# A one-core diffusion layer with 32 streamed experts: reordered and halved weight loads, gate rows moved into the routing, a split first gather, and VectorE's round test moved

## The reference, cut to what matters

```python
h = rmsnorm(x) * (1 + sc_m) + sh_m
mix = mixing_branches(h, ...)
x = x + gt_m * mix
h = rmsnorm(x) * (1 + sc_f) + sh_f
logits = h @ w_router + b_router
g = softmax over the 4 largest of the 32 logits
for e in range(32):
    gate, up = split(h @ w_up[e] + b_up[e])
    y = ((clip(up) + 1) * min(gate, 7) * sigmoid(1.702 * gate)) @ w_down[e] + b_down[e]
    acc += g[:, e] * y
x = x + gt_f * acc
y = rmsnorm(x) * g_final
```

## Time and profile before

| | us |
|---|---|
| runs | 1147.65 median of 3 (1145.46 to 1150.6) |
| the profiled execution | 1146.25 |
| its span, first to last instruction | 1144.4 |
| PE busy in the span | 1070.3 (94%) |
| DVE busy | 332.1 (29%) |
| ACT busy | 169.8 (15%) |
| moved by DMA | 459.37 MB, mean 401 GB/s |

### The profile page before, as it was taken

The page is one execution under the profiler, slowest core; times in us unless marked ns, Lnnn a source line. Parts: engine busy times, 40 slices in busy tenths (PEclk is TensorE's granted clock), DMA queues, the critical chain, the costliest instruction groups (busy, mean ns, idle before and its releaser), DMA issues.

```text
span 1144.4 us, 14105 instructions
## 1 busy us (share of the span) xinstructions
PE 1070.3 (94%) x5882; PEld 505.8 (44%) x5882; DVE 332.1 (29%) x622; ACT 169.8 (15%) x303; POOL 66.4 (6%) x107
## 2 busy tenths in 40 slices
PE   7999899899999999989999999999999999999996
PEld 6877699843333333333333333333333333333332
DVE  4775877522121212121212121212121211211113
ACT  4453145411000000000000000000000000000001
POOL 5050000200000000000000000000000000000000
PEclk9999999999999999999999999999999999999999
DMA  9988977899999999998999999999999999999995
GB/s 308 375 253 341 387 271 319 335 409 406 428 427 434 429 434 434 428 431 365 423 440 431 431 435 426 438 424 439 428 434 432 429 438 424 438 424 438 430 421 221
DMA packets 44056, 459.37 MB, mean 401 GB/s; under 512 B 3668, under 2 KB 16024, under 8 KB 26888
## 3 DMA queue, kind: packets, MB, share of 16 engines
q1 hardware_dynamic: 42376, 455.12, 95.4%
q0 software_dynamic: 1168, 2.81, 1.0%
q10 hardware_dynamic: 464, 0.79, 0.2%
HBM read 457.12 MB, written 1.57 MB: 401 GB/s over the span
## 4 chain that ended last, share of the span: by engine, by line
PE 47%; DMA 45%; DVE 3%; SPq 2%; issue 1%; ACT 1%; POOL 1%; POOLq 0%; DVEq 0%; ACTq 0%
DMA arena<-in_w_down_dram 41%; PE ps L1772 21%; PE ps L1733 12%; DMA ring<-in_w_in_dram 3%; PE ps L1761 2%; PE ps L1713 2%; DMA ring<-in_w_ada_dram 1%; DMA ring<-in_rpb_dram 1%; SPq L427 1%; PE ps L1467 1%; PE ps L1468 1%; PE ps L1635 1%; PE ps L1469 1%; SPq L423 1%; PE ps L1637 1%
## 5 line engine op out<-in xcount | busy, mean ns | idle before, releaser
L1733 PE MATMUL ps<-ring,arena 128*64 128x512 f32 x2048 | 455.1, 594 | 1.7 <-ACT arena L850 0.8
L1772 PE MATMUL ps<-arena,x 128*64 128x512 f32 x992 | 236.7, 633 | 44.6 <-DMA arena<-in_w_down_dram 44.6
L1733 PEld LDWEIGHTS ps<-ring,arena 128*64 128x64 f32 x2048 | 142.5, 137 | 270.6 <-issue 255.3
L1772 PEld LDWEIGHTS ps<-arena,x 128*64 128x64 f32 x992 | 74.8, 145 | 205.0 <-issue 151.0
L1278 DVE TENSOR_SCALAR x<-ps 128x512 f32<-128x512 f32 x32 | 22.1, 692 | 254.8 <-PE ps L1733 254.8
L1293 DVE TENSOR_TENSOR late<-ps,gtf 128x512 f32<-128x512 f32 x64 | 41.2, 686 | 187.6 <-PE ps L1772 187.6
L1271 DVE TENSOR_SCALAR arena<-iota,cur 128x128 f32<-128x128 f32 x64 | 19.3, 345 | 259.9 <-PE ps L1743 256.7
L640 POOL COPY selbuf<-sel 96x64 bf16 (+1 forms) x32 | 24.5, 766 | 848.9 <-DVE x L1279 846.5
L1761 PE MATMUL ps<-late,arena 64*128 64x512 f32 x264 | 65.6, 615 | 1.5 <-DVE late L1293 1.5
L1713 PE MATMUL ps<-arena 128*128 128x128 f32 x512 | 62.7, 276 | 0.0
L862 ACT ACTIVATE x<-x 128x512 f32<-128x512 f32 x32 | 20.1, 630 | 283.4 <-DVE x L1278 283.4
(11 more groups left out here) (267 smaller groups left out, 859.6 us busy)
## 6 DMA issues: line engine op xcount, KB each, us to landing
ring<-in_w_up_dram SPq DMA_DIRECT2D x51, 4096.0 KB, 30.9
arena<-in_w_down_dram SPq DMA_DIRECT2D x26, 4096.0 KB, 20.3
ring<-in_w_up_dram SPq DMA_DIRECT2D x26, 2048.0 KB, 11.5
arena<-in_w_down_dram SPq DMA_DIRECT2D x9, 2048.0 KB, 16.9
ring<-in_w_ada_dram SPq DMA_DIRECT2D x16, 1024.0 KB, 10.6
ring<-in_w_ada_dram SPq DMA_DIRECT2D x16, 512.0 KB, 10.1
ring<-in_w_in_dram SPq DMA_DIRECT2D x16, 512.0 KB, 9.5
ring<-in_w_in_dram SPq DMA_DIRECT2D x8, 1024.0 KB, 7.2
```

The lines of the kernel that those rows point to most:

```text
L1733: ins = mm(ps[CAP * h:CAP * h + CAP, half, :].rearrange("q (p j) -> q p j", j=4), xgT[:, place, kk, CAP * a:CAP * a + CAP], w[:, half, :, ...
L1772: ins = mm(ps[CAP * n:CAP * n + CAP, YB, :], hT[:, j, CAP * h:CAP * h + CAP], w[:, jj, n * HALF:(n + 1) * HALF], start=(jj == 0), stop=(jj ...
```

## The change

Five things are changed. (1) `EVEN_FROM` goes from 10 to 24, so the order with ahead = 4 holds up to expert 23; the load loop issues down(6) to down(21) with the up chunks between, and its body is written in that order. `down` of the experts 28 and 29 is loaded in halves too. (2) The first 1 MB row of `up(2)` is issued by itself once `up(0)` has read its row 0 (`row_free`), the second row behind `moe_free`. (3) gt_f is spread during the routing (`spread_gate`, in the place of `inject(0, 0)`, with 64 output columns a matmul, into banks 4 and 7), and ACT copies it in two instructions ahead of the loads of `b_down`; the second half of `down(0)` waits for it, since it overwrites gt_f's rows. (4) The gather ahead of expert 0 is split in two quarters with a copy each, so that row 0 waits for the first alone; `inject(0, 0)` and `inject(1, 0)` stand ahead of `up(1)`. (5) DVE's test for a further round stands ahead of the last `gated`, and the last scatter has a semaphore of its own.

```diff
-EVEN_FROM, EVEN_TO = 10, E - 4
-LOAD_LOOPS = (EVEN_TO - EVEN_FROM) // LOAD_BODY
+LOAD_FROM, LOAD_TO, EVEN_FROM = 6, 22, 24
+LOAD_LOOPS = (LOAD_TO - LOAD_FROM) // LOAD_BODY
-DOWN_HALVES = [0, 1, 2, 3, E_LAST - 1]
+DOWN_HALVES = [0, 1, 2, 3, E_LAST - 3, E_LAST - 2, E_LAST - 1]
...
+                                if (e, c, h) == (2, 0, 0):
+                                    sp.wait_ge(row_free, r + 1)
+                                    sp.dma_start(up_chunk(2, 0)[:, 0, :], w_up_v[2, :, 0, 0:SLOT])\
+                                        .then_inc(up_loaded[0][0], 16)
+                                    sp.wait_ge(moe_free, R + 1)
+                                    sp.dma_start(up_chunk(2, 0)[:, 1, :], w_up_v[2, :, 0, SLOT:2 * SLOT])\
+                                        .then_inc(row_loaded, 16)
+                                    continue
...
                 for h in range(2):
+                    if h and r == 0:
+                        sp.wait_ge(bc_done, 2)
                     down_part(0, 4 * h, 4 * h + 4, down_loaded[h])
-                fixed(order(2, EVEN_FROM + 2))
+                chunks = order(2, E)
+                starts = [chunks.index(("down", e, None)) for e in (LOAD_FROM, LOAD_TO, E - 2)]
+                fixed(chunks[:starts[0]])
                 with sp.Fori(0, LOAD_LOOPS) as i:
...
-                        for c in range(2):
-                            up_whole(e0 + (h + 2), h, c, at0 + 6 * h)
-                        down_whole(e0 + (h + 1), at0 + 6 * (h + 1))
-                fixed(order(EVEN_TO + 2, E)[:-1])
+                        down_whole(e0 + h, at0 + 6 * h)
+                        up_whole(e0 + (h + 2), h, 1, at0 + 6 * h)
+                        up_whole(e0 + (h + 3), 1 - h, 0, at0 + 6 * (h + 1))
+                fixed(chunks[starts[1]:starts[2]])
...
+            def gate_rows_out():
+                act.wait_ge(bc_done, 2)
+                for t in range(2):
+                    ins = nc.scalar.activation(gate_rows[:, t, :], ps[:, GT_BANK[t], :], ACT.Copy)
                 ins.then_inc(bc_read, 1)
...
-            mod_out(0)
...
             nc.scalar.activation(misc[:, 12:13], mhalf[:, :], ACT.Exp)
+            gate_rows_out()
             act.wait_ge(af_t, 4)
...
+                    for h, (done, ready) in enumerate(((gath_first, xg_first), (gath_done, xg_ready))):
+                        act.wait_ge(done, 1)
+                        nc.scalar.activation(xgT[:, 1, 2 * h:2 * h + 2, :],
+                                             ps[:, FIRST[h], 0:2 * P].rearrange("p (a b) -> p a b", a=2),
+                                             ACT.Copy).then_inc(ready, 1)
...
-                gated(R + E - 1, N + PIECES)
...
             further_rounds(dve, more, run)
+            dve.wait_ge(L["gfin"], 16)
+            gated(E - 1, PIECES)
...
-                dve.wait_ge(last_scat, t + 1)
+                dve.wait_ge(final_scat, t + 1)
...
+            def spread_gate():
+                for t in range(2):
+                    for n in range(2):
+                        q = 2 + n
+                        ins = mm(ps[CAP * n:CAP * n + CAP, GT_BANK[t], :], selrow[32 * q:32 * q + 32, t, 0:CAP],
+                                 modrow[32 * q:32 * q + 32, 2, :], start=True, stop=True)
                 ins.then_inc(bc_done, 1)
...
-            spread(0)
...
-            inject(0, 0)
+            spread_gate()
...
             inject(0, 1)
+            pe.wait_ge(bc_read, 2)
             inject(1, 1)
...
+                if r == 0 and e == 1:
+                    inject(0, 0)
+                    inject(1, 0)
...
                         if kk == 0:
+                            pe.wait_ge(xg_first, 1)
+                        if kk == 2:
                             pe.wait_ge(xg_ready, 1)
-                        if kk == 2:
                             pe.wait_ge(h2_ready, 4)
-                            gather(1, 1, FIRST[1])
+                            gather(1, 1, FIRST[2])
                             totals()
                         if kk == 4:
                             pe.wait_ge(xg_ready, 2)
-                            inject(1, 0)
...
-            gather(1, 0, FIRST[0])
+            pe.wait_ge(oh_ready, 1)
+            for h, done in enumerate((gath_first, gath_done)):
+                for j in range(2 * h, 2 * h + 2):
+                    for t in range(2):
+                        ins = mm(ps[:, FIRST[h], (j % 2) * P:(j % 2 + 1) * P], h2[:, t, j * P:(j + 1) * P], oh[:, t, :],
+                                 start=(t == 0), stop=(t == 1))
+                ins.then_inc(done, 1)
```

More of the change, by code:

```diff
@@ L384, in layer_kernel @@
         NT = [(n, t) for n in range(2) for t in range(2)]
-        AF_BANK = (0, 1, 2, 3)
-        FIRST, AGAIN = (6, 3), (2, 3)
+        AF_BANK, GT_BANK = (0, 1, 2, 3), (4, 7)
+        FIRST, AGAIN = (6, 4, 3), (2, 3)
         def read_flags(eng):
@@ L779, in _, with shift_out @@
             pt_out(2)
-            def mod_out(n):
-                act.wait_ge(bc_done, n + 1)
+            def shift_out():
+                act.wait_ge(bc_done, 1)
                 for t in range(2):
[L786 to L793, removed]
+                    ins = nc.scalar.activation(h2[:, t, :].rearrange("p (a j q) -> p a q j", a=2, j=4),
+                                               ps[:, 2 + 2 * t:4 + 2 * t, :].rearrange("p a (q j) -> p a q j", j=4),
+                                               ACT.Copy)
+                ins.then_inc(bc_read, 1)
+            def gate_rows_out():
+                act.wait_ge(bc_done, 2)
+                for t in range(2):
+                    ins = nc.scalar.activation(gate_rows[:, t, :], ps[:, GT_BANK[t], :], ACT.Copy)
                 ins.then_inc(bc_read, 1)
@@ L878, in experts @@
                 R = r * E
-                for c in range(2):
-                    xg_out(R + 1 + c, c, 1, (AGAIN if r else FIRST)[c])
+                if r:
+                    for c in range(2):
+                        xg_out(R + 1 + c, c, 1, AGAIN[c])
+                else:
+                    for h, (done, ready) in enumerate(((gath_first, xg_first), (gath_done, xg_ready))):
[3 more added lines that the diff above has]
+                                             ACT.Copy).then_inc(ready, 1)
+                    xg_out(2, 1, 1, FIRST[2])
                 if r == 0:
@@ L1330, in run @@
             def run(r):
+                gated(r * E - 1, r * PIECES)
                 dve.wait_ge(last_scat, 2 * r)
@@ L1589, in _, with spread_shift @@
             prob_t(Ss[:, :, P:TOK], 4)
[L1591 to L1598, removed]
+            def spread_shift():
+                pe.wait_ge(cols_read, 3)
                 for t in range(2):
@@ L1601, in spread @@
                         ins = mm(ps[:, 2 * t + q, :], selrow[32 * q:32 * q + 32, t, :],
-                                 modrow[32 * q:32 * q + 32, 2 - n, :], start=True, stop=True)
+                                 modrow[32 * q:32 * q + 32, 1, :], start=True, stop=True)
+                ins.then_inc(bc_done, 1)
+            def spread_gate():
[4 more added lines that the diff above has]
+                                 modrow[32 * q:32 * q + 32, 2, :], start=True, stop=True)
                 ins.then_inc(bc_done, 1)
@@ L1624, in _ @@
                 if j == 4:
-                    spread(1)
+                    spread_shift()
                 if j >= 2:
@@ L1831, in up @@
                         turn_weights(g - 1)
+                    if (e, kk) == (2, 1):
+                        pe.wait_ge(row_loaded, 16 * (r + 1))
                     ins = up_row(e, kk)
+                    if (e, kk) == (0, 0):
+                        ins.then_inc(row_free, 1)
                     if kk % 2:
@@ L1898, in finish @@
                 if r == ROUNDS:
-                    scatter(last, last_scat, 1, True)
+                    scatter(last, final_scat, 1, True)
                 else:
                     with pe.If(more[r - 1] < 1):
-                        scatter(last, last_scat, 1, True)
+                        scatter(last, final_scat, 1, True)
                     with pe.Else():
```

19 lines of the change are left out of this document (10 added, 9 removed).

## The result

The changed kernel takes 1140.56 us (median of 9 runs, 1139.19 to 1143.39) against 1147.65 (9 runs, 1144.43 to 1150.6): a ratio of 0.9943, with a 95% interval of 0.9928 to 0.9957. It is 0.57% faster; the forecast was 1141.2. The profiled execution took 1139.19, with a span of 1137.2, 7.2 us shorter than before.

The account below looks back on a forecast made before the run. From about 400 us the stream of loads, at 432 GB/s, was taken to set the pace. Terms -1.3 - 1.8 - 1.8 - 0.4 - 1.1 = -6.4 gave 1139.85 profiled, 1141.2 on the median's scale; range 1137.9 to 1145.2.

Parts of the forecast that it names:

- gt_f out of the attention output: Attention output: PE loses spread(0), 1.99 us, so the load stream starts sooner; -1.3 us, bounds 0 and -2.0.
- gt_f into the routing: Routing: spread_gate's 1.99 us fills inject(0, 0)'s 1.06 and PE's 0.93 idle; costs nothing, at most 0.2 us.
- down(0): Second half of down(0), issued near 221 instead of 218: loads queued ahead cover 7 us, so cost nothing.
- first row: First row of up(2) goes out some 2.5 us before 230.86; adds stock, not time, counted in the 1.8.
- Split gather and injects: Ahead of up(0) and up(1): PE returns buffers 1.75 us sooner, filling the 243 to 276 hole; -1.8, bounds 0 and -2.6.
- Order: Switch moved from expert 10 to 24: hole shrinks by 2.65 us if down takes 7.11; -1.8, bounds 0 and -2.65.
- the hole only moves: Rival at the switch: down(23) is slow, about 9.8 us, so the switch gives nothing; 1143.0; chance 0.24.
- Halves: down(28) and down(29): PE starts each 4.9 us before its whole load is there; -0.4 us, bounds 0 and -1.3.
- DVE's test: At the end: DVE starts late behind ACT by its branch after the last gated; -1.1 us, bounds 0 and -1.2.
- The front was not hidden: Denies rival: stream start hangs on another step than O_done, or 2 MB loads cause 398 GB/s; 1144.3; chance 0.11.
- A price for each transfer: Rival on loads: each costs a fixed time, so the three added ones cost +4.8 us, 1146.0; chance 0.02.
- The slower case: Rival for fourteen more experts: ahead = 4 feeds the stream at 398 GB/s, +35 us, 1176; chance 0.04.

## Why the prediction was right, point by point

**Bound.** Right: from 400 us on the stream kept 429 to 433 GB/s, and the edits whose worth was shown moved the end by what they did to the stream or behind it. The sum has no term for PE at the end, though, and PE set it with the switch at 28.

**gt_f out of the attention output**, -1.3: right, 1.4 to 1.5. SP's issue of `w_up` gained more, 2.48 us, beyond the 2.0 that was given as the bound, but only 1.4 of it was left at 60 MB; where the rest of it went was not looked into.

**gt_f into the routing**, 0: right (7.94 us against 8.04). It was argued as two idle or movable pieces filled exactly; leaving the place empty showed that the fill also keeps the clock, which the prediction did not see. The second half of **down(0)**, 0: right, PE waits for no load from 245 to 300 us. The **first row** of `up(2)`, 0: right.

**Split gather and injects**, -1.8: right in mechanism, and -2.1 in size. The bracket of 2.44 us ahead of `up(1)` did take both injects and left 0.45.

**Order**, -1.8: the step that failed. "Its size is that of PE's `down` ahead of it" held as far as it went, but the value taken, 7.11 from down(23)'s row, was taken for a property of that place. It is not: the fast and the slow alternate, and the lag of the last transfer comes on top. By the prediction's own figures one queued load of 9.7 us covers a `down` of 9.76 all but for 0.06 us; it had no term for the rest of the hole, of which the lag is 2.45. With the order put back the hole was 1.8 us; with the change it was 1.1 to 3.5. The rival "the hole only moves" describes this part better than the forecast did. Its price, 1143.0, was not met, and yet the kernel with the old order is as fast as the changed one (0.9938, against 0.9943 and 0.9933): the order's own worth can't be told from nothing. The hole of 4.7 us in the profile of before was read as what this order costs; in the other profile with this order it was 1.8. Whether the kernel before has so large a hole in most of its executions is not shown, since it was profiled once.

**Halves** of down(28) and down(29), -0.4: nothing was found. The bound of 0 holds, and so does its reason: PE meets the next wait, 5.4 us for `up`. **DVE's test**, -1.1: right, 1.06 between the two profiles and 0.9 by itself.

The **rivals**. The front was not hidden, and the test is what delayed DVE. A price for each transfer is not to be seen: with down(28) and down(29) whole the rate from 1000 to 1120 us was 426, with them halved 427. The Trainium skill (DMA: Bandwidth & Descriptors, Bandwidth) has larger transfers nearer to the peak, in a table of transfers issued from GpSimd. Behind a filled queue of SyncE the 2 MB ones here show no loss. The slower case, ahead = 4 at 419 GB/s or less, did not occur: 432 in the 370 us that run in it.

The forecast was met within 0.7 us, with gt_f, gather and test, 4.6 us together where 4.2 were forecast, shown one by one. The remaining 2.5 us are not settled: between the two profiles they lie in the hole, which was anywhere from 1.1 to 4.7 us in these profiles, but putting the old order back took nothing away. That the sum came so near is in that part luck.

## What to carry to other kernels

A gap in a stream is an event, not a constant: before an edit is priced by one, look at the same place in a second profile, and ask which of its parts (a clock level, the lag of the last transfer) may come out otherwise. Work taken out of PE may leave it idle and cost time behind it as well: here 1.82 us of idle were followed by 1.36 us more in the two injects, which ran mostly at the lower clock. Once a stream has no hole left, the end may hang on the engine that reads it: check PE's waits behind the spot before another hole is filled.

## What was not expected of the hardware

An idle time of 1.82 us of PE in the routing was followed by 0.61 and 0.50 of the granted clock, and the two injects (16 records) that take 2.03 us took 3.39. From 400 us on, over all fourteen profiles, all 112 `down` behind waits of 1.2 to 1.7 us took 7.09 us; of the 148 behind waits of more than 2.3 us 127 took 8.4 to 10.1, and 21 took 7.09.

The 16 short records that close one load of 4 MB came 1.8 to 4.6 us apart, in a steady pattern over many loads, and the pattern differed between two executions of one kernel. The Trainium skill (DMA: Bandwidth & Descriptors, Why a DMA increments its semaphore by 16 and not by 1) says that a transfer is spread over up to 16 engines that finish independently, and that the semaphore counts them. The trace agrees: PE starts `down` 0.5 us behind the last of the 16 records. How far apart they come the page does not say; here it moved the end of a hole by up to 1.6 us.
